# Four fixed experts dispatched ahead of the expert order, overflow bookkeeping in the expert block, gate weights in four column slices

## What is computed

```python
def hier_moe(u, w_group, b_group, w_inner, b_inner, w1, w3, w2):
    g_logits = (x @ w_group).astype(jnp.float32) + b_group.astype(jnp.float32)
    g_sel = jnp.argmax(g_logits, axis=-1).astype(jnp.int32)
    ...
    vals, idx = lax.top_k(in_sel, TOP_K)
    gate = jax.nn.softmax(vals, axis=-1) * g_w
    expert_id = g_sel[:, None] * EXPERTS_PER_GROUP + idx.astype(jnp.int32)
    return moe_experts(x, expert_id, gate, w1, w3, w2).reshape(shp)
...
        hmid = jax.nn.silu(xblk @ w1[e]) * (xblk @ w3[e])
        return hmid @ w2[e]
...
def ple_add(h, p_i, g, w_gate, b_gate, w_proj):
    gate = jax.nn.sigmoid(rmsnorm(h, g) @ w_gate + b_gate)
    return h + gate * (p_i @ w_proj)
```

## Time and profile before

| | us |
|---|---|
| median of 3 runs | 1465.16 (1464.05 to 1465.61) |
| the profiled execution | 1469.39 |
| its span, first to last instruction | 1467.6 |
| PE busy in it | 1168.2 (80%) |
| DVE busy | 513.4 (35%) |
| mean granted clock of PE | 0.877 |

### The profile page before, as it was taken

The page is one execution under the profiler, slowest core; times in us unless marked ns, Lnnn a source line. Parts: engine busy times, 40 slices in busy tenths (PEclk is TensorE's granted clock), DMA queues, the critical chain, the costliest instruction groups (busy, mean ns, idle before and its releaser), DMA issues. The chain is left out here.

```text
span 1467.6 us, 25425 instructions
## 1 busy us (share of the span) xinstructions
PE 1168.2 (80%) x10797; PEld 762.8 (52%) x10797; DVE 513.4 (35%) x1422; ACT 322.1 (22%) x835; POOL 25.0 (2%) x33
## 2 busy tenths in 40 slices
PE   8999896857849585889988887997876957857777
PEld 7767654534425342467665556664443534424346
DVE  4972612212222121354856551342122212212245
ACT  4573230101101010142233330231110101101133
POOL 0100000000000000001011100000000000000000
PEclk9999998978979787989979995998887978878899
DMA  9644299999999999983034425649999999999970
GB/s 266 209 192 186 115 400 427 426 427 427 426 427 426 427 423 425 422 274 115 1 138 150 166 74 226 251 188 427 427 426 427 427 426 427 426 427 426 425 293 30
DMA packets 61163, 464.11 MB, mean 316 GB/s; under 512 B 17532, under 2 KB 28825, under 8 KB 35422
## 3 DMA queue, kind: packets, MB, share of 16 engines
q1 hardware_dynamic: 58830, 442.95, 73.1%
q0 software_dynamic: 1792, 18.88, 3.5%
q10 hardware_dynamic: 416, 0.53, 0.1%
HBM read 460.80 MB, written 2.49 MB: 316 GB/s over the span
## 5 line engine op out<-in xcount | busy, mean ns | idle before, releaser
L983 PE MATMUL ps<-area,hiddenT 128*32 128x256 f32 x2304 | 191.0, 488 | 204.8 <-issue 201.7
L983 PEld LDWEIGHTS ps<-area,hiddenT 128*32 128x32 f32 x2304 | 89.7, 135 | 287.6 <-issue 261.3
L1691 DVE COPY y<-ps 32x256 f32<-32x256 f32 x140 | 58.3, 417 | 424.2 <-PE ps L983 423.0
L973 PE MATMUL ps<-area,uT 128*32 128x256 f32 x2560 | 161.5, 406 | 19.7 <-issue 8.9
L973 PEld LDWEIGHTS ps<-area,uT 128*32 128x32 f32 x2560 | 92.3, 118 | 85.4 <-issue 31.1
L1631 ACT COPY y<-ps 32x256 f32<-32x256 f32 x140 | 51.0, 364 | 382.4 <-PE ps L983 381.5
L1333 PE MATMUL ps<-sel,u_rows 128*128 128x256 f32 (+3 forms) x480 | 124.5, 386 | 0.2 <-DVE sel L1305 0.2
L973 PE MATMUL ps<-area,xsT 128*32 128x256 f32 x2048 | 124.4, 396 | 0.0
L1749 DVE TENSOR_TENSOR hidden<-silu,ps 128x128 f32<-128x128 f32 x72 | 20.7, 288 | 260.7 <-ACT silu L1647 260.7
L973 PEld LDWEIGHTS ps<-area,xsT 128*32 128x32 f32 x2048 | 75.6, 117 | 47.7 <-issue 12.3
L1333 PEld LDWEIGHTS ps<-sel,u_rows 128*128 128x128 f32 (+1 forms) x480 | 77.1, 187 | 44.3 <-issue 35.1
(11 more groups left out here) (382 smaller groups left out, 1270.6 us busy)
## 6 DMA issues: line engine op xcount, KB each, us to landing
area<-in_w_exp_gate_dram SPq DMA_DIRECT2D x64, 2048.0 KB, 21.9
area<-in_w_exp_up_dram SPq DMA_DIRECT2D x64, 2048.0 KB, 26.2
area<-in_w_exp_down_dram SPq DMA_DIRECT2D x64, 2048.0 KB, 23.3
area<-in_conv_w_in_dram SPq DMA_DIRECT2D x8, 1024.0 KB, 11.9
area<-in_w_ple_gate_dram SPq DMA_DIRECT2D x2, 4096.0 KB, 32.2
area<-in_conv_w_out_dram SPq DMA_DIRECT2D x1, 4096.0 KB, 19.1
area<-in_w_o_dram SPq DMA_DIRECT2D x1, 4096.0 KB, 12.9
area<-in_w_uq_dram SPq DMA_DIRECT2D x3, 768.0 KB, 9.8
```

The source lines that it names most:

```text
L973: last = pe.matmul(s.ps[SLOT * j:SLOT * (j + 1), bank, 0:2 * P].rearrange("p (a f) -> p a f", a=2), xT[:, k, :], up[:, :, k, j * P:(j + 1) ...
L983: last = pe.matmul(s.ps[SLOT * g:SLOT * (g + 1), bank, 0:q], hidden[:, SLOT * j:SLOT * (j + 1)], down[:, j, g * q:(g + 1) * q], start=(j = ...
L1691: last = V.tensor_copy(y[a:a + SLOT, (e // PER) % 2, g * q4:(g + 1) * q4], s.ps[SLOT * g:SLOT * (g + 1), 3 + e % 2, 0:q4])
```

## The change

**Constants.** `FIXED` goes from 3 to 4 and `BEFORE` from 3 to 2, so `ORDER` stays the same list, but turn 3 always belongs to expert 3.

**Route.** From the ranks in PSUM DVE computes for the four fixed experts alone the slot of each token (`early`), zero where the rank is 32 or more, reduces it to `early_rel` and selects with it. The order, the slots and `m.turns` follow behind. The steps `row` and `rel` for the first quad are gone. Ten of twelve fillers are gone. The bookkeeping of overflow blocks leaves the block.

**Experts.** The bookkeeping now opens DVE's program here; a new semaphore `placed` says that it is done, and the engines that read `m.over` or `m.row` wait for it. The tiles that it needs from route lie in `xsT` (`m.other`), which is first written by the dispatch of the second group. That group's selection (`choose(1)`) stands behind turn 0's `hiddenT`, and its first dispatch behind turn 0's down products. SP reads no table for expert 3.

**Gate weights.** Four transfers of 256 columns each, a semaphore for each; PE waits for slice c / 2 ahead of column block c. The block's small tile `gate` lies in `xsT`.

```diff
-FIXED = UPS
+FIXED = 4
 DOUBLES = 4
-BEFORE, BETWEEN = 3, 5
+BEFORE, BETWEEN = 2, 5
...
-                busy(pe, 12)
+                busy(pe, 2)
...
                 dve.wait_ge(s.pe.sem, s.pe.at(3))
+                ranks = s.ps[:, 1, 0:3 * E].rearrange("p (t e) -> p t e", e=E)[:, :, 0:FIXED]
+                link(V.scalar_tensor_tensor(out=early[:], in0=col(s, "iota")[:, FIXED:2 * FIXED]
+                                            .rearrange("p (a e) -> p a e", a=1).broadcast_to([P, 3, FIXED]),
+                                            scalar=float(SLOT), in1=ranks, op0=ALU.mult, op1=ALU.add))
+                link(V.scalar_tensor_tensor(out=early[:], in0=ranks, scalar=float(SLOT), in1=early[:],
+                                            op0=ALU.is_lt, op1=ALU.mult))
+                for k in range(2):
+                    last = V.tensor_tensor(early_sum[:, k], A[:, k, :, 0:FIXED], early[:], ALU.mult)
+                link(last)
+                link(V.tensor_reduce(early_rel[:].rearrange("p (k t) -> p k t", k=2), early_sum[:], AX.X, ALU.add))
+                halves = select(nc, s, m.sel[:, :, P:WIDE], early_rel, 0, P)
+                link(next(halves))
+                next(halves).then_inc(s.sel_ready.sem, 1)
+
                 V.tensor_copy(cum[:].rearrange("p t e -> p (t e)"), s.ps[:, 1, 0:3 * E])
...
-                link(V.scalar_tensor_tensor(out=row[:], in0=beyond[:], scalar=float(SLOT * (TURNS + MAX_OVER)),
-                                            in1=slot[:], op0=ALU.mult, op1=ALU.add))
-                link(V.tensor_tensor(m.rel[:, 0:6], row[:].rearrange("p k t -> p (k t)"),
-                                     col(s, "group_at")[:, 0:1].broadcast_to([P, 6]), ALU.subtract))
-                halves = select(nc, s, m.sel[:, :, P:WIDE], m.rel, 0, P)
-                link(next(halves))
-                next(halves).then_inc(s.sel_ready.sem, 1)
...
-                V.tensor_copy(m.turns[:], m.turns_f[:])
-
-                link(V.tensor_tensor(cmp[:], cnt[:].rearrange("p (e a) -> p e a", a=1).broadcast_to([P, E, 8]),
-                                     col(s, "steps").rearrange("p (a k) -> p a k", a=1).broadcast_to([P, E, 8]),
-                                     ALU.is_gt))
...
-                V.tensor_scalar(m.over[0:1, 0:1], over_end[0:1, E - 1:E], 0.0, None, ALU.add)
+                link(V.tensor_copy(m.turns[:], m.turns_f[:]))
...
         def overflow(engine):
+            engine.wait_ge(s.placed.sem, s.placed.at(1))
             return engine.value_load(m.over[0:1, 0:1], min_val=0, max_val=MAX_OVER)
...
-                    load_up(sp, s, io, p, expert_at(sp, p) + layer * E, s.up_in[p % UPS].sem)
+                    e = expert_at(sp, p) if p >= FIXED else p
+                    load_up(sp, s, io, p, e + layer * E, s.up_in[p % UPS].sem)
...
-                    if fill_at(e) is not None:
+                    if e and fill_at(e) is not None:
                         dispatch(*fill_at(e))
...
                     expert_down(pe, s, down_view(s, p), hidT[:], 3 + e % 2).then_inc(s.down_done.sem, 1)
+                    if e == 0:
+                        dispatch(*fill_at(e))
...
                         widened(0)
+                        act.wait_ge(s.placed.sem, s.placed.at(1))
                         diagonal(m.row)
...
-                choose(1)
+                cmp, nb, over_end, later_at = m.cmp, m.nb, m.over_end, m.later_at
+                tmp, shift, later, owner = m.tmp, m.shift, m.later, m.owner
+                link = chained(dve, s.dve)
+                link(V.tensor_tensor(cmp[:], m.counts[:].rearrange("p (e a) -> p e a", a=1).broadcast_to([P, E, 8]),
+                                     col(s, "steps").rearrange("p (a k) -> p a k", a=1).broadcast_to([P, E, 8]),
+                                     ALU.is_gt))
...
+                V.tensor_scalar(m.over[0:1, 0:1], over_end[0:1, E - 1:E], 0.0, None, ALU.add)\
+                    .then_inc(s.placed.sem, 1)
...
                     turn_hidden(nc, hid, hidT).then_inc(s.h_ready.sem, 1)
+                    if e == 0:
+                        choose(1)
...
+        m.other = sb("xsT", [P, DC, WIDE])
+        room = m.other[:, :, :].rearrange("p c t -> p (c t)")
...
-    sp.dma_start(ple_weights(s)[0], io["w_ple_gate"][layer].rearrange("(k p) n -> p k n", p=P)).then_inc(s.ple_in.sem, 16)
+    w, src = ple_weights(s)[0], io["w_ple_gate"][layer].rearrange("(k p) n -> p k n", p=P)
+    for q in range(4):
+        cols = slice(2 * P * q, 2 * P * (q + 1))
+        sp.dma_start(w[:, :, cols], src[:, :, cols]).then_inc(s.ple_in[q].sem, 16)
...
                 def gate_products(c):
+                    if c % 2 == 0:
+                        pe.wait_ge(s.ple_in[c // 2].sem, s.ple_in[c // 2].at(16))
...
-                pe.wait_ge(s.ple_in.sem, s.ple_in.at(16))
                 gate_products(0)
```

112 lines of the change are left out of this document (66 added, 46 removed).

## The result

The changed kernel takes 1449.71 us, the median of four runs from 1446.84 to 1451.36, against 1465.28 for the kernel before. The ratio of the times is 0.9894, with a 95% interval of 0.9876 to 0.9913: 15.6 us less. The profiled execution took 1450.1 us, with a span of 1448.3.

A forecast was written before the change was run, and what follows sets the result against it. The expert weight stream was taken to bound the kernel, through its start and what follows its last landing. 4.2 + 4.6 + 2 x 0.9 + 2.5 + 2.7 = 15.8 us off 1465.2 gave 1449.4, range 1443.5 to 1457.

The forecast's parts named there:

- Early selection: Route: ranks to `sel` in 2.5 us instead of 7.27; dispatch 4.2 us earlier in layer 0, 4.6 in layer 1.
- First expert load: Start of the expert stage: first load 5.1 us (layer 0) and 5.5 us (layer 1) earlier against the ranks.
- rival (3): Clock falls for the dispatch: 4.3 us in layer 0, 1.7 for layer 1's expert 0; 1455.4 us, chance 0.10.
- Bookkeeping in the expert block: Expert block: `hidden` on time in layer 0, some 1.3 us late in layer 1; later loads covered, cost 0.
- Gate weights in slices: End of each expert stage: PE starts the gate products 2.5 us earlier in layer 0, 2.7 in layer 1.
- SP's margin: Block boundary: SP issues the fourth slice about 1 us ahead; cost 0, a later slice 3.0 us a layer.
- The clock at the gate products: First gate products: idle gap shrinks from 6.3 to 3.7 us but stays, so the low clock's price stays.
- Rival (1): Gate products: the clock survives the shortened gaps, 4.7 us more gain, 1444.7 us; chance 0.15.
- (2): Block boundary: SP is late with its fourth slice and both gate gains go, 1454.6 us; chance 0.10.
- (4): Expert stream: bubble after the first load because expert 1 comes later, 3.3 us a layer, 1456.0 us; chance 0.04.
- (5): Route: stage boundary comes no earlier; only SP's 1.8 and the gate's 5.2 us remain, 1458.2 us; chance 0.03.
- (6): Experts: expert 3 needs an overflow block from its 33rd row, making it slower, 1469 to 1474 us; chance 0.02.

The follow-up runs named there:

- one gate load: The changed kernel with the gate weights in one transfer again, the rest kept: 1455.11 us, ratio 0.9923 to the kernel before.
- the second trace of the changed kernel: The changed kernel run again with no edit: 1449.77 us, ratio 0.9885 to the kernel before.
- The experiment: The changed kernel with the overflow bookkeeping moved back into the route block on DVE, behind the expert order: 1457.28 us.
- the two experiments: The changed kernel with the gate weights in one transfer again, 1455.11 us; the kernel before with only the four slices and their waits added, 1459.82 us.
- the idle pieces filled: The changed kernel with 10 fillers instead of 8 ahead of the ranks and 2 more ahead of the wait for the turned rows: 1450.63 us.
- the boundary filled: The changed kernel with 14 unused products ahead of the gate products and two fillers behind the first dispatch: 1442.52 us.

## Why the prediction was right

The forecast was 1449.4 us, the time is 1449.7. The mechanism was right; that the number is right to 0.3 us is in part luck, as the third point says. By its steps:

- **Early selection.** 2.49 us from the ranks to `sel`, both layers, for 2.5. In layer 1 the dispatch came 7.33 - 2.54 = 4.8 us earlier, for 4.6. In layer 0 it was 5.9 for 4.2. The term was sized with the clock at 0.50 over fillers and the start of the dispatch, as it stood in the earlier trace rows; it stood at 1.00 in this trace, and the fillers took 1.16 us. The run with one gate load shows the case of the low clock, and it is worse than the forecast had it: not the first 1.5 us at the lower clock but all of the dispatch, 6.4 us.
- **SP without the table.** 0.99 us a layer for 0.9, and 1.0 in the experiment that puts the read back.
- **First expert load.** 7.0 and 4.0 us earlier against the ranks, 11.0 in all, for 5.1 and 5.5. In layer 1 the missing 1.5 us are expert 0 at 5.35 instead of 3.66, the small half of rival (3). The two misses, 1.9 too little and 1.5 too much, both come from the granted clock and cancel. That is luck: in the second trace of the changed kernel the loads come 7.0 and 5.7 us earlier, and in the run with one gate load, where the other half of rival (3) came too, 0.1 and 4.0. With expert 0 at 3.66 on both sides the distance is 21.61 before and 15.89 after: 5.7 us, the 4.8 and 0.9 to 1.0 of the two steps.
- **Bookkeeping in the expert block.** Cost 0, as taken. Where expert 0 takes 3.66 us the down products wait 2.16 us for `hiddenT`, 1.0 more than where it takes 5.35 (1.15), for the 1.3 of the forecast. Expert 1's loads are in time all the same, and the stretch from the first load to the last expert is 435.1 and 434.5 us, as before. The second group's dispatch, moved behind the down products, has no run of its own. The experiment shows what the move spares: it would now end the route block by 1.95 us a layer.
- **Gate weights in slices.** 2.56 and 2.65 us for 2.5 and 2.7, and 5.3 and 5.6 us in the two experiments for 5.2.
- **SP's margin.** Here the step failed, though without cost. The forecast had the fourth slice issued 1 us ahead of the boundary; SP was through at 598.78 + 22.14 = 620.92, 4.8 us ahead (4.6 in layer 1). I had put two slices between issue and landing, so that SP would be through when the second has drained, 10.9 us behind the start of the last expert's products; it was after 7.4 and 7.8 us, about when the first should have (4.9 + 3.0 = 7.9), so it seems to have some three under way. With eight slices the margin is gone in both layers, which speaks for the kind of limit that I assumed.
- **The clock at the gate products.** Left in the sum, and it stayed: 6.28 and 6.67 us, with the clock at 0.50 in 626 to 630 and in 1403 to 1407. Rival (1) did not come. The runs show that the pause is its cause, 3.70 us being enough and 0.30 not. The rule of the Trainium skill ("TensorE: Matmul & The Clock Gate", Part 1, on oscillation), that idle gaps bring the clock down and short enough ones do not, agrees with these two; the forecast was right to weigh 3.7 us as long. It does not settle every fall here: at 161 us the clock fell in five traces and not in eight others, behind the same idle pieces of 1.2 and 0.9 us.
- **Rivals (2), (4), (5), (6).** None came: ACT waits 0.28 us at the boundary, GB/s has no dip, the stage boundary moved with the dispatch, and there are 64 up loads.
- **The sum.** 15.8 us forecast and 15.6 in the medians, with an interval of 12.7 to 18.2; the four stretches that the change touches make 16.2 in the traces. Taken out one at a time, the slices are worth 5.3 us, the missing table read 2.0 by its trace, and the early selection 8.3 with the fillers kept: they add up to about the whole, as far as intervals of several us can say. That the profiled spans differ by 19.3 is the middle, 5.4 us, less 2.3 of the first and the last stretch. The forecast took off the 4.2 us by which the profiled execution of before lay above its median, and this was needed: had the forecast been made from that execution alone, it would have missed by 4 us.

## What to carry to other kernels

When a chain ahead of a long transfer is shortened, measure it from its own starting event to the first issue; the two kernels' absolute times carry the clock of everything ahead. Fillers ahead of a wait go or stay with the wait: ten of them less with the wait left in place turned a gain of 8 us over the kernel before into a loss of 9, while with the wait gone they were 6 us of pure delay. And where an engine restarts behind a pause that can't be removed, fill the pause to its end: 14 unused products were worth 4.8 us, a third of what the whole change brought.

## What was not expected of the hardware

- **The lower clock can last through full work.** Behind a pause of 4.2 or 5.1 us, or behind none longer than 1.2 us (one gate load, layer 0), PE ran 15 us of dispatch without a break at 0.50; in most traces the same products took 8.51 us at 1.00.
- **Whether expert 0 runs at 5.35 or 3.66 us is settled by something that no edit ahead of it is shown to control.** Its clock was low in 8 of 14 layers with 2 fillers, 4 of 8 with 12, 1 of 2 with the idle pieces filled, and 0 of 2 with the boundary filled. What decides it stays open.
- **SP's issues seem to be held by more than the bytes.** With four slices of 1024 rows it was through 7.4 and 7.8 us behind the start of the last expert's products, with eight of as many rows of half the size, and as many bytes in all, 12.5 and 13.6. The single gate load of before took it 0.43 us to issue.
- **The same code ahead of the first ranks ends at one of two times**, 159.2 to 159.5 or 160.6 to 161.1 us, in every trace of the study.
